# An encoder trunk on one core: steps reordered where stages change, products paired, the FFN's gating on VectorE and ScalarE

## What is computed

```python
for l in range(2):
    mod = silu(c) @ w_ada[l] + b_ada[l]                 # 2048 x 12288: shifts, scales, gates
    sh1, sc1, g1, sh2, sc2, g2 = split(mod, 6)
    h = rms_norm(x) * (1 + sc1) + sh1
    da_q, da_k, da_v, q_a, kv_a, k_rope, sg_u, sg_v = split(h @ w_in[l])     # 4160 columns
    out_a = diff_attention(...)      # 6 heads, two softmaxes each, ALiBi
    out_b = latent_attention(...)    # 6 heads, low-rank q and kv, rotary key
    out_c = spatial_gating(...)      # 4 groups
    x = x + g1 * (concat(out_a, out_b, out_c) @ w_out[l])
    h = rms_norm(x) * (1 + sc2) + sh2
    a = h @ w_up[l]                                     # 2048 x 11264
    y = conv_b + a * w[2] + shift(a, 1) * w[1] + shift(a, 2) * w[0]
    g, val = split(y, 2)
    x = x + g2 * ((silu(g) * val) @ w_down[l])          # 5632 x 2048
```

## Time and profile before

| | |
|---|---|
| median of three runs | 2568.87 us (2553.85 to 2570.5) |
| profiled execution | 2563.53 us, span 2561.7 us |
| mean TensorE clock granted | 0.970 |
| busy: PE, DVE, ACT, POOL | 96%, 67%, 44%, 20% |
| DMA | 597 MB, mean 233 GB/s; 306 to 320 GB/s in the first 256 us |
| difference `wlo` 128x1024 on DVE (L1538) | x710, mean 1.26 us |
| vector part on DVE (L1532) | x150, mean 1.36 us |
| copy `z` from PSUM on ACT; sum of two halves on DVE (L1550) | 0.38 us; 0.68 us |
| gate on POOL: product, high, low | x44 each, mean 2.05, 0.90, 2.04 us |

### The profile page before, as it was taken

One profiled execution on the slowest core, in us unless ns is written; L12 is line 12 of the kernel. 1 busy time (PEld: TensorE's weight loads), 2 busy tenths in 40 slices (PEclk: granted clock), 3 DMA queues, 4 the chain that ended last, 5 costly groups with the idle time before them and its releaser, 6 DMA issues.

```text
span 2561.7 us, 40001 instructions
## 1 busy us (share of the span) xinstructions
PE 2449.1 (96%) x16368; PEld 2116.4 (83%) x16368; DVE 1727.3 (67%) x2353; ACT 1136.5 (44%) x1594; POOL 502.5 (20%) x544
## 2 busy tenths in 40 slices
PE   6789999989999999999999999898999999999999
PEld 2578888888888888888888889888888888888888
DVE  2334656777668889889975367677766666765765
ACT  2233554345443455344444356534544344444543
POOL 3332320012322133213310121000232002110220
PEclk8799998999999999999999999899999999999999
DMA  9999875577889888898775777556786555656654
GB/s 306 320 306 320 272 260 166 183 229 236 268 269 297 279 262 262 271 297 260 255 231 179 250 219 239 160 161 214 227 274 216 187 184 186 189 186 190 190 176 148
DMA packets 450519, 597.02 MB, mean 233 GB/s; under 512 B 24173, under 2 KB 397985, under 8 KB 450081
## 3 DMA queue, kind: packets, MB, share of 16 engines
q1 hardware_dynamic: 394640, 392.47, 48.2%
q0 software_dynamic: 55296, 201.35, 24.0%
q10 hardware_dynamic: 400, 0.65, 0.1%
HBM read 592.30 MB, written 2.10 MB: 232 GB/s over the span
## 4 chain that ended last, share of the span: by engine, by line
PE 87%; DMA 4%; DVE 3%; issue 3%; ACT 2%; POOL 1%; POOLq 0%; ACTq 0%; SPq 0%; DVEq 0%
PE bank L980 86%; DMA raw<-in_w_in_dram 2%; DMA ada<-in_w_ada_dram 2%; ACT whi L1297 1%; DVE wlo L1538 1%; POOL yv L971 1%; POOL mx L975 1%; DMA rows<-in_b_ada_dram 0%; DVE T L1603 0%; ACT hx L1362 0%; DVE hx L1624 0%; POOL mx L973 0%; DVE r L1588 0%; PE bank L1266 0%; ACT sq L1348 0%
## 5 line engine op out<-in xcount | busy, mean ns | idle before, releaser
L980 PE MATMUL bank<-hx,whi 128*128 128x512 f32 (+1 forms) x4864 | 1381.2, 352 | 29.9 <-DVE hx L1624 18.1
L1538 DVE TENSOR_TENSOR wlo<-raw,whi 128x1024 fp32r<-128x1024 f32 (+2 forms) x774 | 932.2, 1209 | 696.3 <-ACT whi L1297 694.7
L1297 ACT ACTIVATE whi<-raw 128x1024 fp32r<-128x1024 f32 (+2 forms) x774 | 786.9, 1020 | 1158.1 <-PE bank L980 1143.7
L980 PE MATMUL bank<-hx,wlo 128*128 128x256 f32 x3840 | 1088.8, 284 | 9.4 <-DVE hx L1624 9.3
L980 PEld LDWEIGHTS bank<-hx,whi 128*128 128x128 f32 x4864 | 856.8, 191 | 170.4 <-issue 37.4
L980 PEld LDWEIGHTS bank<-hx,wlo 128*128 128x128 f32 x3840 | 734.7, 191 | 20.4 <-issue 17.3
L980 PE MATMUL bank<-mx,whi 128*128 128x512 f32 (+1 forms) x2048 | 628.9, 368 | 5.9 <-DVE mqr L1508 4.9
L980 PE MATMUL bank<-mx,wlo 128*128 128x256 f32 x1728 | 495.6, 287 | 12.6 <-POOL mx L975 12.6
L946 POOL DMA_DIRECT2D ada<-in_w_ada_dram x384 | 254.6, 666 | 1241.4 <-DVE acc L1532 647.2
L980 PEld LDWEIGHTS bank<-mx,whi 128*128 128x128 f32 x2048 | 374.7, 195 | 74.6 <-issue 5.5
L980 PEld LDWEIGHTS bank<-mx,wlo 128*128 128x128 f32 x1728 | 334.8, 194 | 16.3 <-POOL mx L975 14.5
(11 more groups left out here) (159 smaller groups left out, 1286.2 us busy)
## 6 DMA issues: line engine op xcount, KB each, us to landing
ada<-in_w_ada_dram POOLq DMA_DIRECT2D x384, 512.0 KB, 6.1
raw<-in_ffn_w_up_dram SPq DMA_DIRECT2D x352, 512.0 KB, 4.3
raw<-in_ffn_w_down_dram SPq DMA_DIRECT2D x176, 512.0 KB, 3.5
raw<-in_w_in_dram SPq DMA_DIRECT2D x128, 512.0 KB, 5.4
raw<-in_w_out_dram SPq DMA_DIRECT2D x48, 512.0 KB, 5.0
raw<-in_w_out_dram SPq DMA_DIRECT2D x32, 256.0 KB, 3.9
raw<-in_mla_w_uq_dram SPq DMA_DIRECT2D x12, 384.0 KB, 3.6
raw<-in_mla_w_ukv_dram SPq DMA_DIRECT2D x6, 512.0 KB, 4.0
```

The lines of the kernel that those rows point to most:

```text
L980: return pe.matmul(out_, lhsT, rhs, start=start, stop=stop, skip_group_check=True)
L1297: return act.activation(out_, in_, ACT.Copy)
L1538: i_ = tt(dst, src, high.bitcast(F32), ALU.subtract)
```

## The change

- Column pair 11 (`KVA_PAIR`) moves to the early pairs; the rotary key's unit (`kr`) becomes the last of the late ones.
- `win` (other than token pairs) and `wout` products are `paired`. The copies of these `win` pairs move from ScalarE to VectorE as a sum of the two halves, `addz` and `res` get a second accumulation for the second half.
- Where `transition` sums squares, GpSimd adds them up two chunks at a time (`padd`, into `sqa`) for chunks 0 to 13; `ms` multiplies the sum (two matmuls) and chunks 14 and 15. `transition` issues a burst before its first chunks if the next batch is not a vector one.
- The start makes two chunks, then a split, and so on; the first two pairs take turns; chunks 8 to 15 go into the queue beside the last two early units. The first loads of batch 1 wait for weights (`w_loaded`); SP starts at 30 conditioning parts instead of 28.
- Groups in the queues are merged or reordered: head work follows the key statistics at once, `gelu` of the u half goes into `second`, in `out_projection` the gating items come before the latent ones, the latent branch's steps are spread over one group a unit (pace 1), what is left over runs into the second sweep, whose first two pairs take turns. So do the first two pairs of every down pass. The conditioning flush turns only the batches that are due.
- The FFN's gate: product on VectorE, high half on ScalarE, low half on VectorE one unit later (`glo`). Nothing of it is left on GpSimd.

```diff
-EARLY_PAIRS = DAQ_PAIRS + DAK_PAIRS + DAV_PAIRS
-LATE_PAIRS = (KVA_PAIR,) + QA_PAIRS + ("kr",) + SGV_PAIRS + SGU_PAIRS
+EARLY_PAIRS = DAQ_PAIRS + DAK_PAIRS + DAV_PAIRS + (KVA_PAIR,)
+LATE_PAIRS = QA_PAIRS + SGV_PAIRS + SGU_PAIRS + ("kr",)
...
+            groups.append([("ms", l, j, v), ("sq", l, j, v + 1) if v + 1 < n else ("root", l, j)])
...
-        self.items(0, "n1", range(4))
-        self.add("first")
-        self.items(0, "n1", range(4, 8))
...
+        for n in range(4):
+            self.items(0, "n1", (2 * n, 2 * n + 1))
+            self.add("first", min(n + 1, SPLITS))
...
+        a, b = EARLY_PAIRS[:2]
+        order = [(a, 0), (b, 0), (a, 4), (b, 4)] + [(pair, k0) for pair in EARLY_PAIRS[2:] for k0 in (0, 4)]
+        for n, (pair, k0) in enumerate(order):
+            if n == 2:
+                self.ada_over(2, len(order) - 6)
+            if n == len(order) - 2:
+                self.ada_flush()
+                groups = self.item_groups(0, "n1", range(8, 16), 2)
+                self.queue.extend([[("onep", 0, 0, 8, 16)] + groups[0]] + groups[1:])
+            self.unit("win", 0, pair, 0, k0, 4, k0 == 0, k0 == 4, 0)
+            if k0 == 4:
+                for c in range(2):
+                    self.add("copy", 0, pair, c, 0)
...
+                groups = self.stats(l, J_DAK)
+                self.queue.extend([[("banks", (0, 1, 2))] + groups[0]] + groups[1:])
+                self.queue.extend([[("dak", l, 0), ("dakmul", l, 0)],
+                                   [("dak", l, 1), ("dakmul", l, 1), ("dak", l, 2), ("dakmul", l, 2)]])
+                self.queue.extend(self.heads(l, 0, NH, 3))
+                self.queue.extend(self.stats(l, J_O))
...
-        self.pace = len(q) / n * 1.02
...
+        while len(q) > 3:
+            self.put(q.popleft())
+        self.add("banks", (0, 1, 2, 6, 7))
+        order = [(0, 0), (1, 0), (0, 1), (1, 1)] + [(pair, x) for pair in range(2, 8) for x in range(2)]
...
+            if n == 4:
+                assert not q
+                self.add("banks", (0, 1, 2, 3, 6, 7))
+            k0, kt = ((6, 4), (10, 2))[x]
+            self.unit("wout", l, pair, 0, k0, kt, x == 0, x == 1, 1)
+            if x == 1:
+                for c in range(2):
+                    self.add("res", l, "wout", 1, pair, c)
+                self.trunk_squares(l, J_N2, pair)
...
-        ks = (2 * pair, 2 * pair + 1)
-        self.add("sq", l, j, ks[0])
-        self.add("sq", l, j, ks[1])
-        self.queue.extend([[], [("ms", l, j, k) for k in ks]])
+        self.add("sq", l, j, 2 * pair)
+        self.add("sq", l, j, 2 * pair + 1)
+        if pair < 7:
+            self.add("padd", l, j, pair)
+        else:
+            self.queue.append([("ms", l, j, 0), ("ms", l, j, 14), ("ms", l, j, 15)])
...
+        if not self.vector_next():
+            self.burst()
...
+        if b == 1:
+            self.second.append([("glo", l, blk)])
...
+            order = [(pair, k0) for k0 in ks for pair in range(2)] + [(pair, k0) for pair in range(2, 8) for k0 in ks]
+            for pair, k0 in order:
...
-            sp.wait_ge(ada_used, 4 * 7)
+            sp.wait_ge(ada_used, 4 * 8 - 2)
...
+                    if 32 <= m < 32 + ADAS:
+                        pool.wait_ge(w_loaded[(m - 31) // 2], 16)
...
-                    pool.wait_ge(silu_done, num["silu", t[1:]] + 1)
-                    pool.wait_ge(tap_done, num["taps", (l, blk_, 1, 1)] + 1)
-                    pool.tensor_tensor(yv[:, 0:512], yv[:, 0:512], yg[:, 0:512], ALU.mult).then_inc(a_ready, 1)
-                    pool.wait_ge(a_ready, pair + 1)
-                    pool.tensor_copy(to[:, :, 0, :], y2).then_inc(a_high, 1)
-                    pool.wait_ge(a_high, pair + 1)
...
+                    pool.wait_ge(sq_ready, n0 + 2)
+                    if p == 0:
+                        pool.tensor_copy(dst, two).then_inc(sq_added, 1)
+                    else:
+                        pool.wait_ge(sq_added, n)
+                        pool.tensor_tensor(dst, dst, two, ALU.add).then_inc(sq_added, 1)
...
-                            elif x_.what == "win":
-                                i_ = three(b[:, 0:S], wh, wl, hi(hx, k), lo(hx, k), start, stop)
                             elif x_.what == "wout":
-                                i_ = three(b[:, 0:S], wh, wl, mixed(k)[:, 0:S], mixed(k)[:, S:2 * S], start, stop)
-                            elif x_.what == "up":
+                                i_ = paired(b, wh, wl, mixed(k), start, stop)
+                            elif x_.what in ("win", "up"):
                                 i_ = paired(b, wh, wl, both(hx, k), start, stop)
                             else:
...
+                    if pre:
+                        pe.wait_ge(sq_added, num["padd", (l, j, 6)] + 1)
+                        products = [(ones, sqa[:, y * S:(y + 1) * S], P, 0, S) for y in range(2)]
...
+                elif kind == "gate":
+                    act.wait_ge(a_ready, num["gate", t[1:]] + 1)
+                    copy(gated(*t[1:])[:, :, 0, :], yv[:, 0:512].rearrange("p (c n) -> p c n", c=2)).then_inc(a_high, 1)
...
+                    if pair not in TOKEN_PAIRS:
+                        order.after(tt(a, b[:, S:2 * S], a, ALU.add))
                     tt(a, b[:, 0:S], a, ALU.add).then_inc(emptied_dve, 1)
+                elif kind == "copy" and t[2] not in TOKEN_PAIRS:
+                    l, pair, c_, ph = t[1:]
+                    b = wait_full(dve, ("win", *t[1:]))
+                    dve.tensor_reduce(ch(z, 2 * pair + c_), b[:, 0:2 * S].rearrange("p (h n) -> p n h", h=2), AX_X,
+                                      ALU.add).then_inc(emptied_dve, 1)
...
+                elif kind == "gate":
+                    dve.wait_ge(silu_done, num["silu", t[1:]] + 1)
+                    dve.wait_ge(tap_done, num["taps", (*t[1:], 1, 1)] + 1)
+                    tt(yv[:, 0:512], yv[:, 0:512], yg[:, 0:512], ALU.mult).then_inc(a_ready, 1)
+                elif kind == "glo":
+                    to = gated(*t[1:])
+                    dve.wait_ge(a_high, num["gate", t[1:]] + 1)
+                    tt(to[:, :, 1, :], yv[:, 0:512].rearrange("p (c n) -> p c n", c=2), to[:, :, 0, :].bitcast(F32),
+                       ALU.subtract).then_inc(a_low, 1)
...
-                        order.after(stt(xa, b[:, S:2 * S], g, xa, ALU.mult, ALU.add))
+                    order.after(stt(xa, b[:, S:2 * S], g, xa, ALU.mult, ALU.add))
                     stt(xa, b[:, 0:S], g, xa, ALU.mult, ALU.add).then_inc(emptied_dve, 1)
```

More of the change, by code:

```diff
@@ L189, in ada_flush_for @@
                 self.burst()
-        self.turn_now()
+        while any(x[1] < batches for x in self.turns + self.sums):
+            self.tick(9)
     def ada_flush(self):
@@ L494, in place_splits, with splits @@
         steps, split, used = [], 0, 0
-        def splits():
+        def splits(limit=None):
             nonlocal split
-            while split < min(used + SPLITS, len(self.units)):
+            while split < min(limit or used + SPLITS, len(self.units)):
                 steps.append(("hi", split))
@@ L504, in place_splits @@
             if t[0] == "first":
-                splits()
+                splits(t[1])
                 continue
-            if t[0] not in self.EVACS and split:
+            if t[0] not in self.EVACS and split >= SPLITS:
                 splits()
```

149 lines of the change are left out of this document (71 added, 78 removed).

## The result

The changed kernel takes 2528.9 us (median of 4 runs, 2526.5 to 2533.1) where the kernel before took 2565.6 beside it: ratio 0.9865, 95% interval 0.9827 to 0.9904. It is faster by 1.4% and in the range given, but that is half of what was forecast: the profiled span fell by 37.0 us (2561.7 to 2524.7) where the forecast had 72.4.

A forecast was written before the change was run, and what follows sets the result against it. The prediction took TensorE, busy for 96% of the span, to bound the kernel. Its terms, 9.2 + 4.0 + 6.6 + 12.6 + 9 + 13 + 18 = 72.4, took 2563.5 to 2491 us; range 2448 to 2540.

The forecast's parts named there:

- likeliest case: Whole kernel: the forecast itself, a time of 2470 to 2515 us, given a chance of 0.56.
- the middle stays as it is: Rival: latent branch and start save 0, projection's end 5, as dependent steps wait as before; 2526 us, chance 0.21.
- Pairing: Input and output projections: paired products save 0.013 us a group over 712 groups, 9.2 us; the copies on VectorE cost nothing.
- Latent heads to the FFN: Latent heads to the out-projection's end: no gain, VectorE takes over as limit; bounds a gain of 20, a loss of 10.
- Squares: Changes of stage: TensorE's sums of squares go from 16 to 4; only the change into layer 1 counted, 4.0 us.
- Burst: Before both layers' FFNs: conditioning work fills 1.9 us of the wait and saves 1.4 of clock each, 6.6 us.
- Gating: FFN: TensorE's waits on GpSimd's low half at the six passes' ends all go, 12.6 us.
- slower rival: FFN gate: hand-over VectorE to ScalarE to VectorE delays weight splits, 2.3 us a block, 101 us; 2592 us, chance 0.09.
- Start: First 260 us: the new order removes two windows of lost DMA transfer time; 9 us, bounds 0 and 13.
- end of projection 8 in layer 0: Layer 0, last head-group statistics to first out-projection unit: shorter queue hides nearly all of 8.8 us lost; 8 us.
- End of projection, layer 1: Layer 1's end of the projection stage: 5 us, smaller than layer 0's since its projection has more units.
- Latent branch: Latent stretches of both layers: one step a unit saves two thirds of 26 us idle and clock loss, 18 us.

The follow-up runs named there:

- e3: The changed kernel with pairing undone in both projections, copies back on ScalarE and one accumulation a residual: 2520.8 us, ratio 0.9827 to the kernel before.
- e5: e4 with the output projection back to three products of 256 columns and one accumulation a residual: 2509.7 us, ratio 0.9774 to the kernel before.
- e9: e4 without GpSimd's additions of squares, TensorE summing all 16 chunks in both kinds of change of stage: 2526.9 us.
- e10: e4 with 15 of 16 accumulations of the vector parts in batches 4 and 10 narrowed from 1024 to 64: 2505.0 us.
- e4: The changed kernel with the merged group of head work split, three groups as before instead of two: 2519.0 us, ratio 0.9818 to the kernel before.
- e1: The kernel before with only the FFN's gate moved off GpSimd, the down projection in its old order: 2557.7 us, ratio 0.9972.
- e6: e4 with the input projection back to three products and its copies on ScalarE, the output projection still paired: 2522.8 us.

## Why the prediction was right in sign and wrong in size

The sign, the kind of limit and the FFN's part were right; the saving is half of the 72.4 us. The likeliest case (2470 to 2515) was not met. The time lies in the wide range and next to the rival that the middle stays as it is (2526), and both are in part luck: that rival had the latent branch and the start at nothing, which they are not, and knew nothing of the losses by the merged group and the paired output projection, which make up for them. The steps that failed, largest first: layer 1's projection, a term of 5 us without a row of its own, 4.6 of pairing, and the merged group at nothing, 17 us together; the term 0 for the latent heads to the FFN, where layer 0 lost 6.8; and the sizes of start and latent branch, some 14. By steps:

- *Pairing, +9.2.* Mis-sized where it was thought safe and wrong where it was set to nothing. Form and copies together give some 5 us in layer 0's input projection (forecast 3.1) and nothing in layer 1's (forecast 4.6); apart, the form is 3.7 and 3.1, as far as single traces can tell, and the copies "at nothing" lose 3.4 in layer 1. The output projection, counted at +1.6, costs 9.6. The whole pairing makes the changed kernel 8 us slower (e3).
- *Latent heads to the FFN, 0.* In layer 0 the load was right: VectorE's 81.6 us before became 101.0, where 20 were to be added. In layer 1 it was not: 78.2 became 89.7, since 12 vector parts stand there where 16 stood, not two more. The failed step was to set the length equal to VectorE's load over the whole stretch (97.6 in 98.4), as if the engines could shift their work within it. The load is uneven: until 510 us TensorE is the busier one, from 510 to 540 VectorE is full and TensorE waits 6.9 us for its differences, and the whole became 6.8 us longer. The second accumulations are the larger cause (e5: back to 104.0), GpSimd's additions the smaller (e9: 2.6). "TensorE needs only some 85" was wrong too: it needs 95 (1.9 of them the burst), and e5 and e10 stop at 101 to 104.
- *Squares, 4.0.* In the change into layer 1, 5.6 measured (e9). Elsewhere I gave nothing; on e4 layer 1's stretch gains 3.8 and layer 0's loses 2.6.
- *Burst, 6.6.* Measured 3.9 to 5.8, by other reasons: the clock part (2 x 1.4) is nothing, and the change into layer 1 has a burst too, which I had ruled out. The forecast "2.7 us or less of idle" is missed by 0.1 (2.82) before the first FFN.
- *Gating, 12.6.* All six waits went, 11.6 us of span by the turns alone, and nothing more by the move on top of them. The size was right, the cause was not: the step "afterwards product and low half are 0.7 us each" took the instructions' lengths for the gate's, and put both edits into one term, so it could not tell that the turns alone were enough. The gate on VectorE lasts 4.15 us in e1, since others stand between its parts. The slower rival (loss from a delay of 3.2 us on) did not come: product and copy are late by one difference, and ScalarE's next weight split follows its copy at once (1273.37), as the argument against it had said.
- *Start 9 and end of projection 8 in layer 0.* Together with pairing 12.4 of 20.1; without pairing 7.6 to 8.2 of 17 (e3 373.3, e6 372.7, before 380.9). Until 240 us DMA moved 317 GB/s where it had moved 310, which is some 5 us of transfer (an estimate: 7/317 of 240), not 9. Of the two windows of the start only the first was mended; the second is as it was, 0.70 of the DMA engines' time where the earlier trace rows had 0.72:

```profile
160.00:180.00 20.00, 16.08 (x94) 11.62 (x93) 12.71 (x23) 7.56 (x13) 3.04 (x4) 0.83 0.70 220
```

- *End of projection, layer 1, 5.* The term was carried over from layer 0 without a row of its own. In layer 1 TensorE was busy for 240.6 of 242 us before (window 1358 to 1600), so there was nothing to win:

```profile
1358.00:1600.10 242.10, 240.59 (x2032) 220.41 (x2032) 141.56 (x206) 123.61 (x214) 37.29 (x49) 0.99 0.72 225
```

  And the merged group, shown in the diff and not priced, cost 7. With it apart (e4) layer 1's projection takes 242.6 us, what it took before: neither this term nor pairing's 4.6 came.
- *Latent branch, 18.* Saved 13.1 with pairing, 7.5 and 5.6. The clock rose from 0.71 and 0.74 to 0.90 and 0.85 where the branch is prepared, not to 1.00:

```profile
410.00:444.00 34.00, 31.16 (x177) 25.98 (x177) 25.53 (x39) 13.85 (x25) 2.11 (x4) 0.90 0.63 193
...
1619.00:1653.00 34.00, 30.99 (x168) 25.52 (x167) 24.09 (x38) 13.39 (x24) 2.12 (x4) 0.85 0.57 170
```

What stays open: why the start and the latent part gave less than their idle time. No run undid these two alone. Nor is it settled why the paired form should be worth 3 us in the input projections, if it is: a paired group steps 0.347 to 0.356 us there in the median instead of 0.360, but some 26 in each layer take 0.40 us and more, and over all steps under 0.6 us the means are near each other (0.360 to 0.361 against 0.359 to 0.360 in layer 0, 0.357 to 0.360 against 0.360 to 0.362 in layer 1).

## What to carry to other kernels

A change in many parts must be priced edit by edit, also those that look like tidying: here two groups merged into one cost 7 us, and the gate's move gave nothing beside the reordering. When an engine takes over as the limit, compare the engines' loads piece by piece and not over a whole stretch: here VectorE had 101 of 111 us to do, but 29.65 of 30 in one piece, and there TensorE waited. Work that frees one engine (a paired product, a sum on an idle engine) pays only where that engine is the limit. A wait at the end of a pass is removed by reading the late block later; making the late block faster only shortens it.

## What the runs showed of the chip

I had read the earlier trace rows as both engines slowed at once. The traces show that such a pair takes turns: whichever instruction begins second is held, and its listed duration holds the wait. First VectorE held by GpSimd's addition. GpSimd's timeline of the changed kernel, then VectorE's:

```profile
514.25 1.69 POOL L1017 TENSOR_TENSOR r<-r,sq 128x512 f32<-128x512 f32 x1 [1.46 <-ACT sq L1397]
...
521.24 1.69 POOL L1017 TENSOR_TENSOR r<-r,sq 128x512 f32<-128x512 f32 x1 [1.36 <-ACT sq L1397]
```

```profile
513.57 1.22 DVE L1590 TENSOR_TENSOR wlo<-raw,whi 128x1024 fp32r<-128x1024 f32 x1
514.70 2.33 DVE L1584 SCALAR_TENSOR_TENSOR acc<-ada,sml,acc 128x1024 f32<-128x1024 f32 x1
...
517.55 1.27 DVE L1584 SCALAR_TENSOR_TENSOR acc<-ada,sml,acc 128x1024 f32<-128x1024 f32 x1
...
521.69 2.32 DVE L1584 SCALAR_TENSOR_TENSOR acc<-ada,sml,acc 128x1024 f32<-128x1024 f32 x1
```

The additions end at 515.94 and 522.93, VectorE's at 517.03 and 524.01: 1.09 and 1.08 us later, and the one beside nothing took 1.27. The difference of 1.64 us in the earlier trace rows ends 1.08 us after GpSimd's product, in the same way (1003.96 and 1002.88).

The other direction: the addition at 514.25 began while VectorE's difference of 513.57 was running, and ends 1.15 us after it (515.94 and 514.79). All 18 additions of e4 begin so, 0.65 to 0.68 us behind the start of a difference of 1.22, and all last 1.66 to 1.71 us; that they are alike comes from this and does not mean that nothing holds them. GpSimd's product of 2.15 us in the earlier trace rows began 0.23 us behind such a difference, and ends 1.16 us after it (1002.88 and 1001.72), while the one of 1.28 us in the earlier trace rows has no instruction of VectorE beside it:

```profile
1000.50 1.22 DVE L1538 TENSOR_TENSOR wlo<-raw,whi 128x1024 fp32r<-128x1024 f32 x1
```

This is what the Trainium skill states ("SBUF — State Buffer", "Who interferes with whom": the shared port pair is an exclusive lock), and what the prediction set aside; the rule is right here, and the loss is not the full length of GpSimd's instruction, as the prediction had it by the rule, but what is left of it when VectorE's begins.

That the clock falls after the change of stage with 2.8 us of idle as it did with 4.6 was not expected either, nor that a wait of 2.2 us in the projection was followed by 10 us at 0.68 and 0.64.
